# A two-layer diffusion backbone on one Trainium2 core: where the norms' sums, the modulation and the softmax division are done

## The reference, cut to what matters

```
def _modulate(x, g, shift, scale):
    return _rms_norm(x, g) * (1 + scale) + shift
h = _modulate(x, n1, sh1, sc1)
q_na, k_na, v_na, cq, ckv, k_rope = split(h @ w_in)
o = concat(neighbourhood attention (8 heads), latent attention (8 heads)) @ w_out
x = x + g1 * o
x = x + g2 * _grouped_moe(_modulate(x, n2, sh2, sc2), ...)   # 16 experts, top-2 inside one of 4 groups
```

## Time and profile before

| | us |
|---|---|
| median of three runs (1290.98 to 1295.49) | 1291.67 |
| the profiled execution | 1291.43 |
| its span | 1289.6 |
| PE busy in the span | 1138.2 |
| DVE busy | 366.6 |
| ACT busy | 277.4 |
| POOL busy | 103.6 |

### The profile page before, as it was taken

One profiled execution on the slowest core, in us unless ns is written; L12 is line 12 of the kernel. 1 busy time (PEld: TensorE's weight loads), 2 busy tenths in 40 slices (PEclk: granted clock), 3 DMA queues, 4 the chain that ended last, 5 costly groups with the idle time before them and its releaser, 6 DMA issues. The chain is left out here.

```text
span 1289.6 us, 19112 instructions
## 1 busy us (share of the span) xinstructions
PE 1138.2 (88%) x8093; PEld 567.9 (44%) x8093; DVE 366.6 (28%) x884; ACT 277.4 (22%) x673; POOL 103.6 (8%) x111
## 2 busy tenths in 40 slices
PE   4998999984999999999489989999579999999935
PEld 2455466542344444443144545665234444444313
DVE  3102554116122222212140056431512212222214
ACT  1111444113011111111131035430401111111112
POOL 3200000300001101100000010000010101100000
PEclk8999999986999999999679999999779999999975
DMA  9803555343499999998651155531646999999721
GB/s 363 313 16 131 215 196 197 133 175 145 150 368 371 373 373 386 379 376 317 257 188 41 66 197 214 196 131 66 245 151 231 381 366 374 382 387 384 276 107 50
DMA packets 68707, 311.67 MB, mean 242 GB/s; under 512 B 8837, under 2 KB 11105, under 8 KB 46081
## 3 DMA queue, kind: packets, MB, share of 16 engines
q1 hardware_dynamic: 58400, 288.58, 58.6%
q0 software_dynamic: 9344, 18.55, 4.4%
q10 hardware_dynamic: 864, 3.15, 0.6%
HBM read 304.24 MB, written 18.58 MB: 250 GB/s over the span
## 5 line engine op out<-in xcount | busy, mean ns | idle before, releaser
L710 PE MATMUL psum<-arena 128*64 128x512 f32 x512 | 239.0, 611 | 6.3 <-issue 4.9
L713 PE MATMUL psum<-arena 128*64 128x512 f32 x512 | 239.1, 611 | 0.0
L710 PEld LDWEIGHTS psum<-arena 128*64 128x64 f32 x512 | 68.7, 140 | 150.1 <-issue 148.1
L758 PE MATMUL psum<-arena 128*64 128x512 f32 x512 | 126.7, 616 | 2.7 <-ACT arena L1104 2.7
L1428 DVE SCALAR_TENSOR_TENSOR arena<-arena,psum 64x768 f32<-64x768 f32 x32 | 30.3, 948 | 331.2 <-ACT arena L1099 331.2
L721 PE MATMUL psum<-arena 128*32 128x256 f32 x2048 | 117.4, 381 | 0.1
L1099 ACT ACTIVATE arena<-psum 64x768 f32<-64x768 f32 x32 | 25.7, 804 | 314.1 <-PE psum L713 314.1
L721 PEld LDWEIGHTS psum<-arena 128*32 128x32 f32 x2048 | 63.4, 110 | 65.1 <-issue 27.3
L846 PE MATMUL psum<-arena 128*128 128x384 f32 x256 | 83.5, 487 | 1.2 <-PE psum L834 0.6
L987 PE MATMUL psum<-arena 128*128 128x384 f32 x256 | 83.6, 487 | 0.6 <-PE psum L987 0.6
L525 POOL DMA_INDIRECT arena<-token_rows,row_i x32 | 31.0, 970 | 519.4 <-PE psum L693 266.5
(11 more groups left out here) (223 smaller groups left out, 1224.8 us busy)
## 6 DMA issues: line engine op xcount, KB each, us to landing
arena<-in_w_gate SPq DMA_DIRECT2D x64, 1024.0 KB, 10.5
arena<-in_w_up SPq DMA_DIRECT2D x64, 1024.0 KB, 14.9
arena<-in_w_down SPq DMA_DIRECT2D x64, 1024.0 KB, 7.8
arena<-in_w_ada SPq DMA_DIRECT2D x24, 2048.0 KB, 7.8
arena<-in_w_in SPq DMA_DIRECT2D x6, 2048.0 KB, 22.1
arena<-in_w_out SPq DMA_DIRECT2D x4, 2048.0 KB, 7.7
arena<-expert_rows SPq DMA_DIRECT2D x12, 512.0 KB, 8.3
arena<-in_w_in SPq DMA_DIRECT2D x2, 1664.0 KB, 13.1
```

Of the source, the lines that this page charges most:

```text
L710: ins = nc.tensor.matmul(bank[b][0:MAIN, :], hg[:, k, 0:MAIN], wg[half][:, k % 4, :], start=(k == 0), stop=(k == KD - 1))
L713: ins = nc.tensor.matmul(bank[b][MAIN:P, :], hg[:, k, 0:MAIN], wu[half][:, k % 4, :], start=(k == 0), stop=(k == KD - 1))
L758: ins = nc.tensor.matmul(bank[6][MAIN * j:MAIN * j + MAIN, :], hidT[:, c, 0:MAIN], w[half][:, c % 2, 512 * j:512 * j + 512], start=(c == 0 ...
```

## The change

Four edits, made together:

1. **Sums per tile.** The square and the sum of a tile follow the update of that tile: in the output projection TensorE does `norm_sum(2l+1, c-1)` after column block c, and in `combine` `norm_sum(2l+2, k-2)` after the transposes of tile k. The sums go to bank 6, the squares of n = 1, 3 to `xn`.
2. **Spreading.** The wide block is gone. `norm_spread` is four products of the group's 32 rows of ones and reciprocals into four banks; `normalize` reads the four banks. The factor 32 that this brings is taken out in the square root (`scale=1024.0 / D`).
3. **Modulation on three engines** for n = 1, 2, 3: VectorE only normalises; GpSimd modulates the context part of all tiles and the latent part of tiles 3 and 6 (`POOL_LAT`); ScalarE modulates the latent part of the other six. ScalarE's tables are loaded ahead by a small activation (`load_table`): the square root's before the squares, the exponential's after the square root (n = 1, 3) and after the square roots of the low-rank norms.
4. **Attention.** The diagonals are gone. VectorE takes the reciprocal of each head's sum by itself; GpSimd multiplies the head's probabilities (128 x 384 or 128 x 128) by it in place; `turned` waits for that, per head, and is a plain transpose. The reversed order of the neighbourhood queries is undone where ScalarE copies the output.

```
+            def modulate(n):                       # GpSimd
+                l, i = divmod(n, 2)
+                pool.wait_ge(mod_ready, n + 1)
+                for k in range(KD):
+                    pool.wait_ge(xn_ready, KD * n + k + 1)
+                    if k in POOL_LAT:
+                        pool.tensor_scalar(hT[:, k, CTX:TOK], xn[:, k, CTX:TOK], gain[:, i, k, 1:2], mod[:, 3 * i, k, 1:2], ALU.mult,
+                                           ALU.add).then_inc(h_lat_pool, 1)
+                    pool.tensor_scalar(hT[:, k, 0:CTX], xn[:, k, 0:CTX], gain[:, i, k, 0:1], mod[:, 3 * i, k, 0:1], ALU.mult,
+                                       ALU.add).then_inc(h_ctx, 1)
...
+                for u in range(UNITS):             # GpSimd, after the stores of the keys and values
+                    n, c = unit(u)[3], 2 * (u % 2)
+                    for i in range(2):
+                        pool.wait_ge(rsum_ready, 2 * (UNITS * l + u) + i + 1)
+                        p = prob[:, u % 2, i, 0:n]
+                        pool.tensor_scalar(p, p, rsum[:, c + i:c + i + 1], None, ALU.mult).then_inc(scaled, 1)
...
-            def norm_sums(n):
-                for k in range(KD):
...
+            def norm_sum(n, k):
+                pe.wait_ge(sq_ready, KD * n + k + 1)
+                for g in range(4):
+                    ins = nc.tensor.matmul(bank[6][32 * g:32 * g + 32, 256:256 + QUART], ones[:, 0:32],
+                                           squares(n)[:, k, QUART * g:QUART * g + QUART], start=(k == 0), stop=(k == KD - 1))
...
             def norm_spread(n):
                 pe.wait_ge(rstd_ready, n + 1)
-                nc.tensor.matmul(bank[4][:, P:P + TOK], ones, rstd_wide, start=True, stop=True).then_inc(rstd_ps, 1)
+                for g in range(4):
+                    r = slice(32 * g, 32 * g + 32)
+                    ins = nc.tensor.matmul(bank[spread_at(n) + g][:, 0:QUART], ones[r, :], rstd[r, :], start=True, stop=True)
...
                 def turned(u):
                     n = unit(u)[3]
-                    pe.wait_ge(diag_ready, UNITS * l + u + 1)
                     for i in range(2):
+                        pe.wait_ge(scaled, 2 * (UNITS * l + u) + i + 1)
                         if u >= 1:
                             pe.wait_ge(probT_act if i == 0 else probT_dve, UNITS * l + u)
                         for c in range(n // P):
-                            ins = nc.tensor.matmul(bank[4 + i][:, P * c:P * c + P], prob[:, u % 2, i, P * c:P * c + P], diag[:, u % 2, i, :],
-                                                   start=True, stop=True)
+                            ins = nc.tensor.transpose(bank[4 + i][:, P * c:P * c + P], prob[:, u % 2, i, P * c:P * c + P], ident)
...
                         ins.then_inc(wo_ps, 1)
+                        if c >= 1:
+                            norm_sum(2 * l + 1, c - 1)
...
             def norm(n):                           # ScalarE
+                load_table(ACT.Sqrt)
                 for k in range(KD):
-                    nc.scalar.activation(hT[:, k, :], xT[:, k, :], ACT.Square).then_inc(sq_ready, 1)
+                    if n % 2:
+                        act.wait_ge(x_updated, 8 * (n // 2) + k + 1)
+                    elif n:
+                        act.wait_ge(scat_done, 8 * (n // 2 - 1) + k + 1)
+                    nc.scalar.activation(squares(n)[:, k, :], xT[:, k, :], ACT.Square).then_inc(sq_ready, 1)
                 act.wait_ge(ss_ps, n + 1)
...
-                def diagonals(u):
...
+                def reciprocals(u):
+                    c, cs = 2 * (u % 2), 2 * (u % 4)
                     for i in range(2):
+                        dve.wait_ge(exp_ready, 2 * (UNITS * l + u) + i + 1)
+                        v.reciprocal(rsum[:, c + i:c + i + 1], sums[:, cs + i:cs + i + 1]).then_inc(rsum_ready, 1)
```

More of the change, by code:

```diff
@@ L227, in build @@
         part_logits = ada_rows[:, 0:TOK]
[L228 removed]
+        eps_wide = vec[:, 2, 64:65]
+        warm = vec[:, 2, 65:66]
         pad = bias_flat[:, 0:RPB_ROWS * GRID]
@@ L306, in freed_before, with spread_at, squares, quarters @@
             return (ADA_PIECES + 8) * (l + 1) + 4 * (UNITS_E * l + u)
+        def spread_at(n):
+            return 4 if n else 0
+        def squares(n):
+            return xn if n % 2 else hT
+        def quarters(x):
+            return x.rearrange("p (g n) -> p g n", g=4)
+        def lat_wait(eng, n, k):
+            if n == 0:
+                eng.wait_ge(h_lat, k + 1)
+            elif k in POOL_LAT:
+                eng.wait_ge(h_lat_pool, len(POOL_LAT) * (n - 1) + POOL_LAT.index(k) + 1)
+            else:
+                before = sum(1 for j in range(k) if j not in POOL_LAT)
+                eng.wait_ge(h_lat, KD + (KD - len(POOL_LAT)) * (n - 1) + before + 1)
         def two_banks(b):
@@ L356, in overflow, with unit @@
                     eng.sem_inc(s, share)
+        def unit(u):
+            kind, r = divmod(u, 12)
+            pair, t = divmod(r, 3)
+            return kind, pair, t, (P if t == 0 else TOK)
         @block.sync
@@ L551, in experts @@
                     scatter(units[-1])
+                modulate(2 * l + 1)
                 pool.wait_ge(rows_ready, l + 1)
@@ L643, in release @@
                 pe.sem_inc(slot_free, 1)
-            def norm_sums(n):
-                for k in range(KD):
[L647 to L651, removed]
+            def norm_sum(n, k):
[3 more added lines that the diff above has]
+                                           squares(n)[:, k, QUART * g:QUART * g + QUART], start=(k == 0), stop=(k == KD - 1))
+                if k == KD - 1:
+                    ins.then_inc(ss_ps, 1)
             def norm_spread(n):
                 pe.wait_ge(rstd_ready, n + 1)
-                nc.tensor.matmul(bank[4][:, P:P + TOK], ones, rstd_wide, start=True, stop=True).then_inc(rstd_ps, 1)
+                for g in range(4):
+                    r = slice(32 * g, 32 * g + 32)
+                    ins = nc.tensor.matmul(bank[spread_at(n) + g][:, 0:QUART], ones[r, :], rstd[r, :], start=True, stop=True)
+                ins.then_inc(rstd_ps, 1)
             def ada_piece(l, j):
@@ L806, in combine @@
                     ins.then_inc(scat_ps, 1)
+                    if k >= 2:
+                        norm_sum(2 * l + 2, k - 2)
+                for k in range(KD - 2, KD):
+                    norm_sum(2 * l + 2, k)
             for l in range(DEPTH):
-                norm_sums(2 * l)
                 if l == 0:
+                    for k in range(KD):
+                        norm_sum(0, k)
                     ada_piece(0, 0)
@@ L1169, in outputs @@
                     act.wait_ge(o_ps, UNITS * l + w + 1)
-                    nc.scalar.activation(hT[:, 4 * kind + pair, P * t:P * t + P], bank[6][:, 0:P], ACT.Copy).then_inc(o_ready, 1)
+                    o = hT[:, 4 * kind + pair, P * t:P * t + P]
+                    if kind == 0:
+                        o = bass.AP(o.tensor, o.offset + P - 1, [list(o.ap[0]), [-1, P]])
+                    nc.scalar.activation(o, bank[6][:, 0:P], ACT.Copy).then_inc(o_ready, 1)
                 exps(0)
@@ L1270, in norm @@
                 norm_scale(n)
-                dve.wait_ge(mod_ready, n + 1)
-                for k in range(KD + 1):
-                    if k < KD:
-                        normalize(n, k)
-                    if k >= 1:
-                        modulate(n, k - 1)
+                for k in range(KD):
+                    normalize(n, k)
             def final_norm():
@@ L1554, in _ @@
                     n = unit(u)[3]
-                    diagonals(u)
+                    reciprocals(u)
                     if u + 2 < UNITS:
```

71 lines of the change are left out of this document (33 added, 38 removed).

## The result

The changed kernel takes 1332.13 us (median of 4 runs, 1325.61 to 1334.64) against 1293.58 for the kernel before (four runs, 1290.98 to 1295.62): ratio 1.0291, 95% interval 1.0247 to 1.0335. It is slower by 39 us; 1258 was predicted. The profiled execution took 1332.83, its span is 1331.0, 41.4 us longer than before.

What follows compares the result with a forecast made beforehand. TensorE bounds the experts; VectorE's chain paces or is level with large attention units; norms are unhidden chains. Attention 16.7 plus norms 17.3 save 34.0 us: 1291.4 to 1257.4, stated as 1258, range 1245 to 1286.

Steps and rivals of the forecast that it cites:

- p = 0.52: Attention, large units: GpSimd's product on one head takes 0.52 us (copy's rate 0.34, fixed 0.07, 0.11 extra); saves 16.7 us.
- the rival with p = 1.3: Attention: GpSimd's start and end costs make each head's product 1.3 us; 1312 us in all; chance 0.1.
- its own ceiling of 43 us: Largest saving of the whole change: 24 us in attention plus 19 in the norms.
- 1.56 - 2p: Saving in us per large attention unit, p being GpSimd's time per head: chain 2.14 before, 0.58 + 2p after.
- the clock falls: Attention: transposes not counting as busy cost the high clock, one round in four, 16 us; 1274; chance 0.05.
- the signs of being wrong that the prediction named: TensorE waits over 1 us a unit; projection much over 2.2 longer; `combine` over 1.5; attention clock under 0.95; experts awaiting weights.
- Predicted 17.3: All norms together save 17.3 us: norms 1 and 3 8.6, norm 2 4.3, norm 4 4.4.
- update to router: Norms 1 and 3, last x update to router's result: 6.5 us saved each, before the cost of sums.
- sums in the projection: Output projection: seven sums in TensorE's order, hidden by nothing, cost 2.2 us for each of norms 1 and 3.
- `combine`: Sums between the transposes of `combine` charged at 0.6 us, for norm 2 and for norm 4.
- Attention saves nothing though p is small: VectorE's copy between `maxes` and the next reciprocals holds the attention unit; only the norms count: 1274; chance 0.1.
- GpSimd's turn-round: Attention: each GpSimd instruction pays an unseen start and end, two in series in 32 units; slower; chance 0.1.

Runs made afterwards that it cites:

- kernels 2, 6: Changed kernel with GpSimd's product given a second factor of one (2), 1275.58 us; with that for the second head only, first head one-factor (6), 1307.80 us.
- kernels 4 and 5: Changed kernel with the product on VectorE instead of GpSimd (4), 1258.64 us; with unread TensorE products filling its waits for GpSimd (5), 1312.37 us.
- experiment 1: Kernel before with edits 1 to 3 (norms) alone, attention as before: 1279.59 us, ratio 0.9882.

## Why the prediction was wrong, step by step

**The step that failed is the price of GpSimd's product.** It said: "The new instruction has one tensor to read, like the copy [...]: p = 0.52", bounded by 0.41 and 0.90. It is 1.245 as written (and 0.66 with a second factor). The bounds came from a copy, a memset and a product of two tensors, and the upper one was taken as the worst because it reads more; but the cost depends on the form of the instruction, and no row of before had this form. The page cited there (the Trainium skill, GPSIMD Engine Reference, Engine selection) warns of operations with two inputs and holds one-input ones to be about line rate; here the one-input, one-factor product (1.26) is dearer than the two-tensor product (1.00) and takes three times VectorE's 0.42 for the same product. The measurement decides. The range for an operation that the trace does not show was too narrow, and the rival with p = 1.3, which gave 1312, had 0.1. Even that rival, with nearly the right price, stopped 20 us short of the result; the clock, below, is most of that. The stated range had a small slip too: its own ceiling of 43 us leads to 1248, not 1245.

**The chain was right where the clock stayed up.** In latent rounds at 1.00, half of what a round gained or lost is 0.35 us a large unit with two factors, -0.23 with one slow head and -0.81 as changed. The prediction's 1.56 - 2p gives 0.24, -0.345 and -0.93 with the measured prices: each step in price is passed on in full, and the line lies 0.11 to 0.12 too low, which no run explains. Over the whole attention it holds less well (both layers; us saved):

| kernel | two products in series | 32 x (1.56 - sum) | measured | mean granted clock |
|---|---|---|---|---|
| product on VectorE | 0.84 | 23.0, at most 20.5 by TensorE | 18.3 | 0.98, 1.00 |
| two factors | 1.32 | 7.7 | 4.8 | 0.99, 0.95 |
| one slow head | 1.905 | -11.0 | -23.1 | 0.88, 0.88 |
| as changed, filled | 2.49 | -29.8 | -35.7 | 1.00, 1.00 |
| as changed | 2.49 | -29.8 | -50.7 | 0.82, 0.80 |

**The clock was costed for the wrong cause.** The rival "the clock falls" blamed the transposes. It does fall, but from TensorE's waits: kernels 2, 6 and the changed one give TensorE the same instructions and differ only in how long it waits (0.99 and 0.95, 0.88 twice, 0.82 and 0.80), and kernels 4 and 5 keep every transpose at 0.98 to 1.00. It takes 15.0 us in attention by the filled kernel (50.7 - 35.7), which is the least, since some filling comes on top; beyond the chain as predicted the changed kernel loses 50.7 - 29.8 = 20.9. The Trainium skill (TensorE: Matmul & The Clock Gate, PE-mode transpose) holds that a transpose does not count as busy in the same way; no run here shows a loss by the 224 transposes. The prediction priced a wait by its length alone, never by what it does to the work around it. By the profiled executions the miss is 34.0 + 41.4 = 75.4 us: 46.5 are the price (64 x (1.245 - 0.52)), 20.9 what attention lost beyond it (at least 15.0 of that the clock), 4.7 the norms, 3.4 the rest. Of the signs of being wrong that the prediction named, three came in attention and `combine`: TensorE waiting for GpSimd over 1 us a unit (0.99 and 0.91 for the two heads above), the clock under 0.95, `combine` longer by 1.9 in layer 1.

**The norms were right in mechanism, and too high in size by a seventh to over a third.** Predicted 17.3; 15.0 by the medians of experiment 1, 12.6 by its stages. Term by term, in that kernel: first normalise 2.85 us after the update (3.3 predicted); update to router 5.9 saved (6.5); sums in the projection 2.5 (2.2); norm 2 4.6 saved (4.9), norm 4 5.4 (5.0); `combine` 1.9 and 2.4 (0.6). The largest error is `combine`: the trace had shown its transposes at the low clock, and there the sums of a tile take 0.55 us, with nothing to hide them, since TensorE's transposes already set the pace: 1.31 us a tile where the earlier trace rows show 0.87 (1.74 for two). Inside the changed kernel the projection was dearer still (4.1, 3.6), since part of it ran at the low clock behind attention.

**The other rivals.** "Attention saves nothing though p is small" is refuted by kernel 4. GpSimd's turn-round is small: a pair ends and TensorE's loads start 0.05 us later. What sets the sign is the engine's time for the instruction itself.

**Open.** Why the one-factor form costs three times as much an element was not looked into. What decides when the clock falls is open as well: latent rounds of the changed kernel with the same work were granted 1.00 and 0.76, and the two-factor kernel lost its 0.95 in layer 2 in the first round (0.85) and the last (0.84) alone.

## What to carry to other kernels

An elementwise operation moved to an engine that has never run its exact form has no upper bound in the trace: measure the form by itself first, in idle time, with its neighbours in form beside it. A wait on the engine that bounds a stage costs more than its length once that engine's clock falls with it (here 50.7 us, against 35.7 with the idle time filled and 29.8 by the chain: 40 to 70% more); a test with the idle time filled tells the two apart. Small sums for a reduction belong where the engine waits anyway, behind the last block, not between blocks that it works off without a gap.

## What was not expected of the hardware

GpSimd's product with one factor takes 1.24 to 1.26 us for 128x384 and 0.60 to 0.62 for 128x128, and 0.66 and 0.45 when a second operation with a second factor is added, in place or not; no run had its neighbours quiet. While it works, a pair of VectorE's 128x128 products takes up to 1.12 instead of 0.48. VectorE does the 128x384 product in 0.42. A 128x384 copy on GpSimd takes 0.525, where 4096 elements of 32 partitions had suggested 0.41. TensorE's mean clock in attention went from 1.00 over 0.99 and 0.95 to 0.88 and then 0.82 and 0.80 as its waits grew, and back to 1.00 when the waits were filled with unread products, with a shorter stage to show for it.
